# Score steps at other places of the block, and half of the probability masks on VectorE, in a hybrid pooling, convolution and attention layer

## The chip, the cores and the metric

The kernel runs on one core of one Trainium2 chip. The metric is the device time of one execution in microseconds. All matrix work is done in pairs of rounded values: each float32 operand is split into a high part and the rest (`hi` and `lo`), and a product is the sum of hi·hi, lo·hi and hi·lo.

## The reference

One layer over 4096 tokens of width 1024, with three groups of heads side by side. Only the attention group is touched by the change:

```
h = rms_norm(x, ln_g)
proj = h @ w_in                      # 1024 x 2816, split into u, g_pool, a, b, g_conv, q, k, v, g_attn
y_pool = pool_mixer(...)             # trailing means of 2/4/8/16 tokens
y_conv = conv_module(...)            # 31 taps, layer norm, silu, pointwise
# q: 8 heads of 64, k and v: 2 heads; each block of 128 queries sees its own and the previous 128 keys
scores = q_block @ [k_previous, k_own] * 64**-0.5 + alibi      # banded: 0 <= distance < 128
p = softmax(concat(scores, sink))[..., :-1]
y_attn = p @ [v_previous, v_own]
y = concat(y_pool * silu(g_pool), y_conv * silu(g_conv), y_attn * silu(g_attn))
out = rms_norm(x + y @ w_out, final_g)
```

## The kernel before

The program has three stages, one after the other. Each engine runs a list of its own, written out by hand, and waits on semaphores; no scheduler moves anything. The first stage (until about 656 us) is the **attention stage**, and only it is changed. Then come the mixer stage (projections of the pooling and convolution groups) and the output projection.

The attention stage goes over 8 blocks `n` of 512 tokens. In a block TensorE makes ten projections by `project`: `k`, `q0` to `q3`, `v`, and the gates `g0` to `g3`, each of 24 matmuls of 512 columns (8 slices `kk` of the 1024 inputs, three products each). The four q projections go to the PSUM tile `wide`, the others in turn to two banks `pair0` and `pair1`. It makes scores by `scores(n, j)` for four subtiles `j` of 128 queries, and the product of probabilities and values by `attend(n, batch)` for two subtiles at a time.

The way of one subtile goes over all engines:

- `scores` on TensorE, into the same PSUM tile as the q projections (tile `wide`).
- `take_scores(n, j, kv)` on VectorE, for 4 heads at a time: a predicated copy (L1034), four sums with the bias and a row maximum (L1038), and two small instructions (L1043, L1044).
- `exps` on ScalarE (L906, L909), `invert` on VectorE (L1055, L1058), `normalise` on GpSimd (L845).
- `turn_squares_of_probs` on VectorE (L1063) transposes the probabilities in squares of 32; `store_probs` and `load_probs` on the SP queue write them to DRAM (L690) and read them back turned (L699).
- `mask(n, j)` on GpSimd zeroes what lies outside the band: four instructions on 64 partitions x 512 columns (L855, L856, twice), two for the early and two for the late half of the queries. The semaphore `masked` counts them, and `attend` waits for it.
- `output(n, batch)` on VectorE multiplies the result by the gate (L1183) and writes `y_out`.

The input of the next block is prepared inside the block: `st.load` loads x, `square` (ScalarE) and `square_more` (VectorE) sum the squares, `fold_sums` is a small matmul on TensorE (L276) placed inside a projection, `mean` on VectorE and `root` on GpSimd (L288) follow, then `scale` on ScalarE (L294) and `turn_squares` on VectorE (L301) for four parts, then `split_hi` on ScalarE (L333) and `split_lo` on VectorE (L339) for 8 slices. The tile `xT` has one buffer: slice `kk` of the next block may be written only when `g3` of this block has read it (semaphore `spent`), and the next block's `k` reads slice by slice what is written.

In blocks 1 to 6 the combinations of the output weights (`combos`, 28 items, up to five a block) are made beside this: a sum on VectorE (L488), the high part on ScalarE (L496), the rest on VectorE (L500), and a store from SP (L506). Their staging tile has two buffers, so an item waits for the landing of the store of the item two before it.

The order in a block of TensorE: `k`, `q0`, `attend(n-1, 0)`, `q1`, `q2` (with the fold in it), `q3`, `v`, `attend(n-1, 1)`, then `scores(n, j)` and `g`j for j = 0 to 3, `turn_v` inside `scores(n, 1)`. Before the scores TensorE waits for all q rests (`q_taken`, made by `make_q_lo` on VectorE after `q_hi` on ScalarE). The last block ends with `attend(7, 0)`; `attend(7, 1)` stands in the mixer stage after its first two projections.

## Time and profile before

| what | value |
|---|---|
| time, median of 3 runs | 1454.54 us (1451.94 to 1455.07) |
| the profiled execution | 1452.87 us, its span 1450.7 us |
| TensorE matmul busy | 1363.4 us, 94% of the span |
| VectorE busy | 1170.9 us, 81% |
| ScalarE busy | 549.3 us, 38% |
| GpSimd busy | 504.8 us, 35% |
| DMA | mean 159 GB/s |

The span is the time from the first to the last instruction of the program; the device time of the same execution is 2.2 us more. Busy shares are means over the three stages. From 750 us on TensorE is busy nearly all the time; the idle time of TensorE lies in the attention stage, so the rows below are of that stage. A row of the timeline gives start, duration, engine, line, operation, and in brackets the idle time before and who ended it.

### The profile page before, as it was taken

How to read it: one execution, taken by the hardware profiler on the slowest of the kernel's cores; microseconds unless marked ns; L12 is line 12 of the kernel's file. 1: busy time of each engine (PE TensorE's matmuls, PEld its weight loads, DVE VectorE, ACT ScalarE, POOL GpSimd, SP SyncE). 2: the span in 40 equal slices, each digit the busy share in tenths (PEclk: the TensorE clock that was granted, in tenths of full speed). 3: DMA queues.
4: the chain of work that ended last, by engine and by line, in shares of the span. 5: the costliest groups of instructions: out<-in, count | busy, mean ns of one | idle time of the engine just before them, and what ended most of it. 6: DMA issues, size and time to landing. Idle time of an engine off the chain costs nothing.

```text
span 1450.7 us, 20622 instructions
## 1 busy us (share of the span) xinstructions
PE 1363.4 (94%) x7070; PEld 1112.5 (77%) x7070; DVE 1170.9 (81%) x2365; ACT 549.3 (38%) x1421; POOL 504.8 (35%) x640
## 2 busy tenths in 40 slices
PE   6989898989989899876999999999999999999998
PEld 5867676767778687755888888888888888888886
DVE  4877768685868675554989999989899998888886
ACT  5746555555555554330221221121222243333332
POOL 5254545445354534552010010110101255555552
PEclk9999999999999999988999999999999999999999
DMA  9757482939384736657031230330326756545531
GB/s 214 218 125 263 124 284 89 288 110 268 124 254 153 203 146 162 245 130 222 12 131 54 108 131 24 136 130 14 131 88 250 286 193 213 164 158 163 159 126 73
DMA packets 112426, 230.78 MB, mean 159 GB/s; under 512 B 16464, under 2 KB 74192, under 8 KB 104656
## 3 DMA queue, kind: packets, MB, share of 16 engines
q1 hardware_dynamic: 88192, 205.85, 42.5%
q10 hardware_dynamic: 24144, 23.80, 6.8%
q8 instruction: 49, 0.80, 0.2%
q14 instruction: 41, 0.34, 0.1%
HBM read 131.05 MB, written 98.57 MB: 158 GB/s over the span
## 4 chain that ended last, share of the span: by engine, by line
PE 66%; DVE 14%; DMA 8%; ACT 5%; POOL 3%; issue 2%; SPq 1%; POOLq 0%; ACTq 0%; DVEq 0%
PE wide L346 12%; PE wide L347 12%; PE wide L348 12%; DMA xs<-in_x_dram 5%; PE pair L1239 3%; PE pair L1233 3%; PE pair L1234 3%; DVE m_tail L1994 3%; DVE a_rows L1038 2%; ACT a_rows L909 2%; PE wide L1233 2%; PE wide L1234 2%; PE turn L1202 2%; PE wide L1239 2%; PE turn L347 2%
## 5 line engine op out<-in xcount | busy, mean ns | idle before, releaser
L1994 DVE SCALAR_TENSOR_TENSOR m_tail<-m_tail,m_taps 128x512 f32<-128x512 f32 x480 | 338.5, 750 | 4.6
L1233 PE MATMUL pair<-xT,w_hi 128*128 128x512 f32 x384 | 154.5, 402 | 27.0 <-ACT xT L333 23.5
L845 POOL TENSOR_SCALAR a_rows<-a_rows,a_inv 128x128 f32<-128x128 f32 x256 | 108.4, 443 | 204.1 <-DVE a_inv L1058 204.0
L1736 POOL TENSOR_TENSOR operand_sums<-m_y 128x512 f32<-128x512 f32 x75 | 102.2, 1362 | 167.7 <-PE wide L348 116.6
L108 POOL TENSOR_TENSOR pool_carrier<-pool_carrier 128x1 f32<-128x1 f32 x23 | 14.0, 611 | 394.5 <-DVE m_meanvar L2003 394.5
L1234 PE MATMUL pair<-xT,w_lo 128*128 128x512 f32 x384 | 150.8, 393 | 0.0
L1239 PE MATMUL pair<-xT,w_hi 128*128 128x512 f32 x384 | 149.2, 394 | 0.9 <-DVE xT L339 0.7
L346 PE MATMUL wide<-x_first,w_hi 128*128 128x512 f32 x320 | 125.4, 392 | 0.0
L346 PE MATMUL wide<-xT,w_hi 128*128 128x512 f32 x320 | 125.2, 391 | 0.0
L348 PE MATMUL wide<-x_first,w_hi 128*128 128x512 f32 x320 | 124.6, 389 | 0.0
L348 PE MATMUL wide<-xT,w_hi 128*128 128x512 f32 x320 | 124.5, 389 | 0.0
L347 PE MATMUL wide<-x_first,w_lo 128*128 128x512 f32 x320 | 124.5, 389 | 0.0
L347 PE MATMUL wide<-xT,w_lo 128*128 128x512 f32 x320 | 124.5, 389 | 0.0
L1233 PEld LDWEIGHTS pair<-xT,w_hi 128*128 128x128 f32 x384 | 72.5, 189 | 51.4 <-ACT xT L333 20.5
L1823 ACT ACTIVATE x_first<-operand_sums 128x512 fp32r<-128x512 f32 x80 | 50.5, 633 | 153.9 <-POOL operand_sums L1736 152.6
L1233 PE MATMUL wide<-xT,w_hi 128*128 128x512 f32 x256 | 103.9, 406 | 0.0
L1234 PE MATMUL wide<-xT,w_lo 128*128 128x512 f32 x256 | 102.5, 400 | 0.0
L1239 PE MATMUL wide<-xT,w_hi 128*128 128x512 f32 x256 | 102.1, 399 | 0.0
L909 ACT ACTIVATE a_rows<-a_rows,a_negmax 128x128 f32<-128x128 f32 x256 | 98.8, 387 | 0.0
L1239 PEld LDWEIGHTS pair<-xT,w_hi 128*128 128x128 f32 x384 | 72.5, 189 | 20.2 <-DVE xT L339 5.2
L1234 PEld LDWEIGHTS pair<-xT,w_lo 128*128 128x128 f32 x384 | 72.6, 189 | 12.3
L1038 DVE CUSTOM_DVE_ANT_0 a_rows<-wide,a_bias,a_sinks 128x128 f32<-128x128 f32 x256 | 74.6, 349 | 2.3
(262 smaller groups left out, 3233.8 us busy)
## 6 DMA issues: line engine op xcount, KB each, us to landing
xT_scratch<-xT SPq DMA_DIRECT2D x16, 2048.0 KB, 10.3
p_scratch<-a_rows SPq DMA_DIRECT2D x32, 512.0 KB, 2.6
x_first<-xT_scratch SPq DMA_DIRECT2D x16, 1024.0 KB, 8.7
xT<-xT_scratch SPq DMA_DIRECT2D x16, 1024.0 KB, 9.0
combo_scratch<-stage SPq DMA_DIRECT2D x28, 512.0 KB, 5.3
m_y<-y_scratch ACTq DMA_DIRECT2D x14, 1024.0 KB, 6.6
xs<-in_x_dram SPq DMA_DIRECT2D x20, 512.0 KB, 10.7
a_pT<-p_scratch SPq DMA_DIRECT2D x64, 128.0 KB, 4.7
```

The costliest lines, as they stand in the source:

```text
L346: nc.tensor.matmul(out, w_hi, x_hi, start=first, stop=False)
L347: nc.tensor.matmul(out, w_lo, x_hi, start=False, stop=False)
L348: return nc.tensor.matmul(out, w_hi, x_lo, start=False, stop=last)
L845: last = nc.gpsimd.tensor_scalar(probs[b][:, h], probs[b][:, h], inv[:, b, h:h + 1], 0.5, ALU.mult, ALU.mult)
L909: last = nc.scalar.activation(probs[b][:, h], probs[b][:, h], ACT.Exp, bias=negmax[:, b, h:h + 1], accum_out=rowsum[:, b, h:h + 1])
L1038: last = nc.vector.tensor_tensor_reduce(out=probs[b][:, h], in0=in_runs(score[:, h, P:]), in1=in_runs(bias[:, h]), scale=1.0, scalar=sinks ...
L1233: nc.tensor.matmul(out, w.hi(c)[:, kk, cols], st.hi[:, kk, :], start=(kk == 0), stop=False)
L1234: nc.tensor.matmul(out, w.lo(c)[:, kk, cols], st.hi[:, kk, :], start=False, stop=False)
L1239: last = nc.tensor.matmul(out, w.hi(c)[:, kk, cols], st.lo[:, kk, :], start=False, stop=(kk == KT - 1))
L1736: nc.gpsimd.tensor_tensor(operand_sums[:, i, 1], y_block(q, left), y_block(q, right), SIGN[op]).then_inc(operand_sum, 1)
L1823: nc.scalar.activation(operands[:, i, 0], operand_source(q, i), ACT.Copy).then_inc(operand_hi, 1)
L1994: nc.vector.scalar_tensor_tensor(out=conv[:, i, :], in0=h[:, i, j:j + TB], scalar=taps[:, i, j:j + 1], in1=conv[:, i, :], op0=ALU.mult, op ...
```

## The change

Four things are moved, all in the attention stage.

**TensorE.** `attend(n-1, 0)` comes before `q0` instead of after it. `scores(n, 0)` comes right after `q3`, before `attend(n-1, 1)` and `v`. `scores(n, 1)` stands in the middle of `g0`, `scores(n, 2)` after `g1`, `scores(n, 3)` in the middle of `g3`, and the next block's `k` at the end of the body. In the last block the scores of 1, 2, 3 stand before `g0`, `g1`, `g2`. The fold is moved from `q2` to `q3`.

**Masks.** GpSimd keeps the two instructions for the early queries (`mask_early`), and `mask_late` on VectorE makes the other two. Both add to `masked`, whose count per subtile stays two. On GpSimd the masks of subtiles 0 and 1 stand after `normalise` of 1 and 2, those of 2 and 3 ahead of `root`.

**VectorE and ScalarE** get a new order for the rest of the block: `output` directly after `make_k_lo`, the late masks of 2 and 3 among the q rests, the four `turn_squares` of x in the gates' part of the block instead of among the q rests, `scale` on ScalarE likewise, the first four splits ahead of the last subtile's scores, the other four behind it, as before.

**SP** stores the probabilities of subtile 3 after it has loaded those of subtile 2, and loads x first.

```diff
@@ SP, body(n)
+                st.load(sp, n + 1, (0, 1))
+                load_probs(sp, n - 1, 2)
                 store_probs(sp, n - 1, 3)
-                st.load(sp, n + 1, (0, 1))
-                for j in (2, 3):
-                    load_probs(sp, n - 1, j)
+                load_probs(sp, n - 1, 3)
@@ GpSimd
-        def mask(n, j):
+        def mask_early(n, j):
             m, b = SUB * n + j, j % 2
             pool.wait_ge(p_loaded[b], 16 * RUNS * (m // 2 + 1))
-            for late in range(2):
-                part = runs(whole[b][:, late * D // 2:(late + 1) * D // 2], halves[late])
-                nc.gpsimd.tensor_tensor(runs(rest[b], halves[late]), part, over_heads(rest_mask, halves[late]), ALU.mult)
-                nc.gpsimd.tensor_tensor(part, part, over_heads(whole_mask, halves[late]), ALU.mult).then_inc(masked, 1)
-                pool.wait_ge(masked, 2 * m + late + 1)
+            part = runs(whole[b][:, 0:D // 2], halves[0])
+            nc.gpsimd.tensor_tensor(runs(rest[b], halves[0]), part, over_heads(rest_mask, halves[0]), ALU.mult)
+            nc.gpsimd.tensor_tensor(part, part, over_heads(whole_mask, halves[0]), ALU.mult).then_inc(masked, 1)
@@ ScalarE, body(n), for the blocks between the first and the last
+            if not final:
+                st.scale(act, n + 1, 0)
+            for kv in range(KV):
+                exps(n, 0, kv)
+            take_v()
+            if not final:
+                st.scale(act, n + 1, 1)
+            for kv in range(KV):
+                exps(n, 1, kv)
+            spread_v()
+            gate_tanh(n, 0)
+            if not final:
+                st.scale(act, n + 1, 2)
+                gate_tanh(n, 1)
+                exps(n, 2, 0)
+                exps(n, 2, 1)
+                st.scale(act, n + 1, 3)
+                gate_tanh(n, 2)
+                for kk in range(st.AHEAD):
+                    st.split_hi(act, n + 1, kk)
+                exps(n, 3, 0)
+                gate_tanh(n, 3)
+                exps(n, 3, 1)
@@ VectorE, body(n)
             make_k_lo(n)
+            if not first:
+                output(dve, n - 1, 0)
                 turn_squares_of_probs(SUB * n - 1)
...
-                if t == 1 and not first and not final:
+                if t == 3 and not final:
                     st.mean(dve, n + 1)
                 make_q_lo(n, t)
...
                 make_combos(n, (t,) if t < 3 else (3, 4))
+                if t > 1 and not first:
+                    mask_late(dve, n - 1, t)
...
+            take_scores(n, 0, 0)
+            take_scores(n, 0, 1)
             if not first:
                 output(dve, n - 1, 1)
+            inverts(0)
+            next_x(0)
+            take_scores(n, 1, 0)
+            turn_squares_of_probs(SUB * n)
+            take_scores(n, 1, 1)
+            next_x(1)
+            inverts(1)
+            gate_make(n, 0)
+            if not final:
+                next_x(2)
+                gate_make(n, 1)
+                take_scores(n, 2, 0)
+                turn_squares_of_probs(SUB * n + 1)
+                take_scores(n, 2, 1)
+                inverts(2)
+                mask_late(dve, n, 0)
+                next_x(3)
+                gate_make(n, 2)
+                for kk in range(PIECE):
+                    st.split_lo(dve, n + 1, kk)
+                for kv in range(KV):
+                    take_scores(n, 3, kv)
+                turn_squares_of_probs(SUB * n + 2)
+                mask_late(dve, n, 1)
+                gate_make(n, 3)
+                inverts(3)
@@ the end of VectorE's attention program
         output(dve, NB - 1, 0)
+        for j in (2, 3):
+            mask_late(dve, NB - 1, j)
+
+    def mask_late(dve, n, j):
+        m, b = SUB * n + j, j % 2
+        dve.wait_ge(p_loaded[b], 16 * RUNS * (m // 2 + 1))
+        part = runs(whole[b][:, D // 2:], halves[1])
+        nc.vector.tensor_tensor(runs(rest[b], halves[1]), part, over_heads(rest_mask, halves[1]), ALU.mult)
+        nc.vector.tensor_tensor(part, part, over_heads(whole_mask, halves[1]), ALU.mult).then_inc(masked, 1)
@@ TensorE, body(n)
-                project(n, "k")
-                project(n, "q0")
                 attend(pe, n - 1, 0)
-            for name in ("q1", "q2", "q3", "v"):
-                project(n, name, folding(n) if name == ("q3" if first else "q2") and not final else None)
+            for name in ("q0", "q1", "q2", "q3"):
+                project(n, name, folding(n) if name == "q3" and not final else None)
             pe.wait_ge(q_taken, GROUP * (n + 1))
+            scores(n, 0)
             if not first:
                 attend(pe, n - 1, 1)
-            for j in range(SUB):
-                scores(n, j, turn_v if j == 1 else None)
-                project(n, f"g{j}")
+            project(n, "v")
+            if final:
+                scores(n, 1, lambda: turn_v(n))
+                project(n, "g0")
+                scores(n, 2)
+                project(n, "g1")
+                scores(n, 3)
+                project(n, "g2")
+                project(n, "g3")
+                attend(pe, n, 0)
+            else:
+                project(n, "g0", halfway(lambda: scores(n, 1, lambda: turn_v(n))))
+                project(n, "g1")
+                scores(n, 2)
+                project(n, "g2")
+                project(n, "g3", halfway(lambda: scores(n, 3)))
+                project(n + 1, "k")
```

Three places show what this does to the order. The first is TensorE after the last q projection of a block. Before, `v` (in `pair`) and the 32 products of `attend` (L1202) stand between `q3` and the scores (L1262, L1271):

```order
L1239 MATMUL pair<-xT,w_hi 128x512
L1202 MATMUL turn<-a_pT,a_v 64x128 x8
L1202 MATMUL turn<-a_rows,a_v 64x128 x8
L1202 MATMUL turn<-a_pT,a_v 64x128 x8
L1202 MATMUL turn<-a_rows,a_v 64x128 x8
L1262 MATMUL wide<-a_k_lo,a_q 128x256 x8
L1271 MATMUL wide<-a_k_hi,a_q 128x256 x8
```

Now the scores (L1294, L1303) follow the last matmul of `q3` (in `wide`), and `attend` (L1234) follows them:

```order
L1271 MATMUL wide<-xT,w_hi 128x512
L1294 MATMUL wide<-a_k_lo,a_q 128x256 x8
L1303 MATMUL wide<-a_k_hi,a_q 128x256 x8
L1234 MATMUL turn<-a_pT,a_v 64x128 x8
L1234 MATMUL turn<-a_rows,a_v 64x128 x8
L1234 MATMUL turn<-a_pT,a_v 64x128 x8
L1234 MATMUL turn<-a_rows,a_v 64x128 x8
L1265 MATMUL pair<-xT,w_hi 128x512
```

So nothing stands any more between `q3` and the scores, which need its rests. The second place is VectorE from the rests of `q3` (`a_q`) to the first scores of the block. Before:

```order
L1083 SCALAR_TENSOR_TENSOR a_q<-wide,a_q 64x512 x2
L301 STREAM_TRANSPOSE xs<-xs 128x1024
L488 TENSOR_TENSOR stage_sum<-raw 128x512 x2
L500 TENSOR_TENSOR stage<-stage_sum,stage 128x512 x2
L301 STREAM_TRANSPOSE xs<-xs 128x1024
L1183 TENSOR_TENSOR y_out<-turn,a_gate 128x2x4x64 x2
L1034 COPY_PREDICATED wide<-a_rows,wide 128x4x128
```

Now, with the late masks of subtile 2 (L1205, L1206, in `a_pT`) and of subtile 3 (in `a_rows`):

```order
L1205 TENSOR_TENSOR a_pT<-a_pT,a_rows 64x512
L1206 TENSOR_TENSOR a_pT<-a_pT,a_rows 64x512
L282 TENSOR_SCALAR a_meansq<-turn 128x16
L1084 SCALAR_TENSOR_TENSOR a_q<-wide,a_q 64x512 x2
L488 TENSOR_TENSOR stage_sum<-raw 128x512 x2
L500 TENSOR_TENSOR stage<-stage_sum,stage 128x512 x2
L1205 TENSOR_TENSOR a_rows<-a_rows 64x512
L1206 TENSOR_TENSOR a_rows<-a_rows 64x512
L1035 COPY_PREDICATED wide<-a_rows,wide 128x4x128
```

The two combinations stay where they were, and the mask of subtile 3, for which `attend(n-1, 1)` waits, stands behind them. The third place is VectorE at the turn from one block to the next. Before, behind the last scores, with the splits of the next block's x (L339):

```order
L1063 STREAM_TRANSPOSE a_rows<-a_rows 128x1024
L339 SCALAR_TENSOR_TENSOR xT<-xs,a_gain,xT 128x512
L1093 SCALAR_TENSOR_TENSOR a_gate<-a_tanh,pair 128x512
L339 SCALAR_TENSOR_TENSOR xT<-xs,a_gain,xT 128x512 x3
L1055 TENSOR_TENSOR a_denom<-a_rowsum,a_sinkexp 128x4
L1058 RECIPROCAL a_inv<-a_denom 128x4
L339 SCALAR_TENSOR_TENSOR xT<-xs,a_gain,xT 128x512 x4
L1063 STREAM_TRANSPOSE a_rows<-a_rows 128x1024
```

Now, behind the last scores:

```order
L1064 STREAM_TRANSPOSE a_rows<-a_rows 128x1024
L1205 TENSOR_TENSOR a_rows<-a_rows 64x512
L1206 TENSOR_TENSOR a_rows<-a_rows 64x512
L1094 SCALAR_TENSOR_TENSOR a_gate<-a_tanh,pair 128x512
L1056 TENSOR_TENSOR a_denom<-a_rowsum,a_sinkexp 128x4
L1059 RECIPROCAL a_inv<-a_denom 128x4
L1056 TENSOR_TENSOR a_denom<-a_rowsum,a_sinkexp 128x4
L1059 RECIPROCAL a_inv<-a_denom 128x4
L339 SCALAR_TENSOR_TENSOR xT<-xs,a_gain,xT 128x512 x4
L1071 COPY a_k_lo<-a_k_lo 128x2x128
```

The first four splits have moved ahead of the last subtile's scores; the last four stand behind both of its scores, a transpose, a mask and a gate.

## Rows read from the trace of the kernel before

**Rows 1.** The waits of TensorE, 50 to 720 us: total us, times, longest

```profile
PE turn L1202 <- POOL a_rows L856: 25.6, 3, 11.1
PE pair L1233 <- ACT xT L333: 23.5, 14, 1.7
PE turn L276 <- ACT a_tanh L239: 13.7, 6, 2.7
```

**Rows 2.** Timeline of TensorE at a block's turn: start, duration, x count, idle before

```profile
319.26 0.47 PE L1233 MATMUL pair<-xT,w_hi 128*128 128x512 f32 x1 [1.61 <-ACT xT L333]
...
323.73 0.50 PE L1233 MATMUL pair<-xT,w_hi 128*128 128x512 f32 x1 [1.74 <-ACT xT L333]
...
327.59 0.40 PE L1233 MATMUL wide<-xT,w_hi 128*128 128x512 f32 x1
...
333.17 1.09 PE L1202 MATMUL turn<-a_pT,a_v 128*64 128x128 f32 x16
...
336.11 0.50 PE L1233 MATMUL wide<-xT,w_hi 128*128 128x512 f32 x1
...
345.96 0.36 PE L276 MATMUL turn<-a_sumsq,a_fold 128*128 128x16 f32 x2 [2.74 <-ACT a_tanh L239]
```

**Rows 3.** Timeline of TensorE at the first scores of block 3

```profile
287.47 0.73 PE L1262 MATMUL wide<-a_k_lo,a_q 64*128 64x256 f32 x8
...
289.19 0.39 PE L1233 MATMUL pair<-xT,w_hi 128*128 128x512 f32 x1
```

**Rows 4.** ScalarE's first instruction behind `k`, all blocks: min/median/max ns, first and last start

```profile
L934 ACT ACTIVATE a_k_hi<-a_k_hi x7: 417/418/421, 95.8 to 560.6; 128x256 fp32r<-128x256 f32 x7
```

**Rows 5.** A stretch behind a fold: length, busy us PE, PEld, DVE, ACT, POOL, granted clock, DMA

```profile
190.10:193.50 3.40, 3.40 (x10) 2.73 (x11) 2.26 (x5) 1.47 (x3) 2.71 (x1) 0.50 1.06 454
```

**Rows 6.** Timeline of TensorE, the last two products of probabilities and values

```profile
640.24 1.98 PE L1202 MATMUL turn<-a_pT,a_v 128*64 128x128 f32 x16 [9.53 <-POOL a_rows L856]
...
667.28 1.98 PE L1202 MATMUL turn<-a_pT,a_v 128*64 128x128 f32 x16 [11.11 <-POOL a_rows L856]
```

**Rows 7.** Groups of VectorE, 0 to 650 us: x count, busy us, mean ns, idle before

```profile
L1038 DVE CUSTOM_DVE_ANT_0 a_rows<-wide,a_bias,a_sinks 128x128 f32<-128x128 f32 x256 | 74.6, 349 | 2.3
L1083 DVE SCALAR_TENSOR_TENSOR a_q<-wide,a_q 64x512 fp32r<-64x512 f32 x64 | 44.1, 689 | 39.2 <-ACT a_q L898 38.0
L1034 DVE COPY_PREDICATED wide<-a_rows,wide 128x512 f32<-128x512 uint32 x62 | 42.2, 681 | 0.0
L339 DVE SCALAR_TENSOR_TENSOR xT<-xs,a_gain,xT 128x512 fp32r<-128x512 f32 x56 | 40.2, 769 | 0.0
L1063 DVE STREAM_TRANSPOSE a_rows<-a_rows 128x1024 f32<-128x1024 f32 x32 | 39.5, 1234 | 8.6 <-POOL a_rows L845 8.6
L301 DVE STREAM_TRANSPOSE xs<-xs 128x1024 f32<-128x1024 f32 x28 | 34.4, 1231 | 1.5 <-ACT xs L294 1.3
...
L488 DVE TENSOR_TENSOR stage_sum<-raw 128x512 f32<-128x512 f32 x20 | 15.6, 778 | 6.1 <-DMA combo_scratch<-stage 3.7 <-DMA raw<-in_w_out_dram 2.0
L500 DVE TENSOR_TENSOR stage<-stage_sum,stage 128x512 fp32r<-128x512 f32 x20 | 15.1, 754 | 11.2 <-ACT stage L496 11.0
```

**Rows 8.** Groups of ScalarE, 0 to 650 us

```profile
L909 ACT ACTIVATE a_rows<-a_rows,a_negmax 128x128 f32<-128x128 f32 x256 | 98.8, 387 | 0.0
...
L294 ACT ACTIVATE xs<-xs,a_rstd 128x256 f32<-128x256 f32 x112 | 47.5, 496 | 1.6 <-POOL a_rstd L288 1.3
...
L333 ACT ACTIVATE xT<-xs,a_gain 128x512 fp32r<-128x512 f32 x56 | 35.7, 709 | 0.0
```

**Rows 9.** A mask group of GpSimd, 0 to 690 us

```profile
L856 POOL TENSOR_TENSOR a_pT<-a_pT,a_rows 64x512 f32<-64x512 f32 x32 | 41.0, 1280 | 0.0
```

**Rows 10.** Timeline of VectorE among the combinations of block 3

```profile
277.26 1.35 DVE L500 TENSOR_TENSOR stage<-raw,stage 128x512 fp32r<-128x512 f32 x1 [1.48 <-ACT stage L496]
...
284.05 0.69 DVE L488 TENSOR_TENSOR stage_sum<-raw 128x512 f32<-128x512 f32 x1 [0.98 <-DMA combo_scratch<-stage]
```

**Rows 11.** The combination's store issued at 264.4 us beside xT's: x count, KB, us to landing

```profile
xT_scratch<-xT SPq DMA_DIRECT2D x1, 2048.0 KB, 10.7
combo_scratch<-stage SPq DMA_DIRECT2D x1, 512.0 KB, 11.6
```

More of the change, by code:

```diff
@@ L957, in body @@
             q_hi(n, 2)
-            if not first and not final:
-                st.scale(act, n + 1, 0)
             for s in combos.of_block(n, (2,)):
@@ L965, in body @@
                 w.split_hi(act, CHUNK_CB)
[L966 to L967 removed]
             q_hi(n, 3)
[L969 to L971 removed]
+            for s in combos.of_block(n, (3, 4)):
                 combos.split_hi(act, s)
@@ L1284, in folding, with turn_v, halfway @@
             return once
+        def turn_v(n):
+            pe.wait_ge(free(slot("v")), earlier(n, slot("v")) + 1)
+            need(pe, gated, batches_before(n, 0))
+            for s in range(SUB):
+                last = nc.tensor.transpose(turn[1][:, s * P:(s + 1) * P], vT[:, s * P:(s + 1) * P], ident[:])
+            last.then_inc(v_turned, 1)
+        def halfway(action):
+            return lambda kk: action() if kk == KT // 2 - 1 else None
         def body(n):
-            first = isinstance(n, int) and n == 0
+            first, final = n == 0, n == NB - 1
             if first:
```

153 lines of the change are left out of this document (55 added, 98 removed).

## The prediction

> **What bounds the kernel now.** I read first the busy shares: TensorE is the fullest engine, and its gaps are all in the attention stage. So the next view is who ends TensorE's waits there [rows 1]: the masks on GpSimd (25.6 us, three waits at the end of the stage), the splits of x at each block's turn (23.5 us), the fold (13.7 us). The timeline shows them in place [rows 2]: `k` waits 1.61 and 1.74 us for ScalarE's splits, the fold 2.74 us for the squares. A block lasts (560.6 - 95.8)/6 = 77.5 us [rows 4]. Its own work on TensorE is ten projections of 5.5 us (327.59 to 333.17 is one), two `attend` of 2.9 (333.17 to 336.11) [rows 2], four scores of 1.7 (287.47 to 289.19) [rows 3] and 0.6 for turning `v`: 68.4 us. The other 9 us are the waits and the clock: behind a fold's wait the granted clock is 0.50 for 3.4 us [rows 5], that is 1.2 instead of 2.4 GHz and some 1.6 us lost, in four blocks. At the end `attend` waits 9.53 and 11.11 us [rows 6], and runs at the low clock again.
>
> **The change, worked out over one block.** Set K = 0 where `k`'s last matmul ends, and follow a block from 1 to 5 until the next K. The sum is made against the profiled execution, 1452.9 us (1.7 us under the median).
>
> *TensorE to the end of q3.* 2.9 for `attend(n-1, 0)`, four projections 22.1, the fold 0.3: 25.3. The fold stands 5.5 us later, and the longest wait for it was 2.74 [rows 2], so it costs nothing now: x is still loaded at the block's turn. Its cover is gone only if x lands more than 3 us later than before. Gain 2.3 us a block, and the low clock with it.
>
> *The rests of q3.* Before, `v` and an `attend` (8.4 us) covered them. Now the scores follow at once and need ScalarE's two copies and VectorE's two rests (0.69 each [rows 7]): with the copies first, 2.1 us of idle time at least, scores at 27.4 to 29.1.
>
> *What VectorE does around it.* Between the rests of q3 and the mask of subtile 3 stand two combinations: four instructions of 0.7 to 0.8 (L488, L500 [rows 7]), then the late mask. No row shows a mask on VectorE. The nearest are the two-input instructions of 512 columns there, 0.69 to 0.75 on average and 1.35 for the one that ran beside GpSimd's masks [rows 7, 10]; against GpSimd's 1.28 [rows 9]. I take 0.68, 1.35 for the pair, since GpSimd has finished its own by then; the bounds are 1.3 and 2.7. That ends the mask at 27.3 + 2.7 + 1.35 = 31.3 if nothing waits, and `attend(n-1, 1)`, which TensorE could start at 29.1, waits 2.2.
>
> *The store that comes into it.* A combination waits for the landing of the store two before it. The block's first store is issued behind 2 MB of xT and lands 11.6 us later [rows 11]. SP now comes to it after the load of subtile 3, which waits for that subtile's store; I put it at 15, its landing at 26.3. The third combination then starts at 26.3 instead of 22.4, and it stands ahead of q3's rests on both engines: the scores slip to 31.3. The fifth waits for the third's store (one such wait of 0.98 shows before [rows 10]), and the mask ends at 37.1. So `attend(n-1, 1)` starts between 31.3 and 37.1; from there 2.9 + 5.5 (`v`) + 2.75 (half of g0) = 11.2 to `scores(n, 1)`.
>
> *From scores(n, 1) to the next K.* TensorE's own work is 30.4 us: the scores with `v` 2.2, half of g0 2.75, g1 5.5, scores 1.7, g2 5.5, g3 with scores 7.2, k 5.5. VectorE's list in the same stretch: 1.3 until the first scores are there; six `take_scores` of 2.07 (0.68 + 4 x 0.35 with the overlaps and two small ones) 12.4; three transposes of probabilities and three of x at 1.15 net, 6.9; two masks 2.7; four gates 2.6; eight splits of 0.72 (0.77 on average, beside GpSimd) 5.8; the inverses 1.5: 33.2 [rows 7]. In it are four waits for ScalarE that nothing covers: for the exponentials of the scores just taken (4 x 0.39 + 0.2 each) before the two inverses, 0.6 and 1.8, for the tanh behind the turned `v` 1.0, for a scale (4 x 0.5) 0.9 [rows 8]: 4.3. Together 37.5. The last splits, which `k` must have, stand behind the last scores, a transpose, a mask and a gate. So `k` ends 7.1 us later than TensorE alone would make it, against about 4.4 before. VectorE's 5.4 us of masks a block lie on this path; GpSimd, which is relieved of them, was off it.
>
> The period is then 31.3 + 11.2 + 37.4 = 79.9 without store waits, 85.7 with them. The landing of 11.6 us [rows 11] makes the second the nearer; I take 84.5, that is 7.0 us more than 77.5 in each of five blocks: +35. Block 6 has no fourth and fifth combination: +0.2 to +4, I take +3. Block 0: `root` (2.9 us) now comes after the last weights, and the scale is ahead of the first exponentials: +5.
>
> *The last block and the end.* The wait before `attend(6, 1)` goes (the weights' loads have one projection more to pass), `attend(7, 0)` has two projections more between it and its scores: I count 2.1 for q3's rests, 1.1 for scores 3, 3.8 before `attend(7, 0)` (the mask behind the last gate), 8.6 before the last one. The last is 11.11 [rows 6] less two mask instructions of 1.28 [rows 9]; its loads are issued as late as before. That is 15.6 for 31.4 (25.6 of waits [rows 1], 5.3 of low clock, 0.5), with some 2 of low clock left: -14, between -10 and -18.
>
> The sum: 35 + 3 + 5 - 14 = **+29 us**, at the median 1484.
>
> *A rule of the chip's notes.* VectorE's instruction with two SBUF inputs took 1.35 us beside GpSimd's masks instead of about 0.7 [rows 10]. The Trainium skill, page "SBUF — State Buffer", section "Who interferes with whom", says the same: an instruction of VectorE with two SBUF inputs contends with one of GpSimd that reads SBUF, and one waits for the other to end. The late masks are of this form, so moving them makes them such a rival of what GpSimd keeps. By that rule one of a block's four masks, that of subtile 0 (GpSimd scales probabilities then), would take up to 1.3 us more: 7 times, +9 at most.
>
> **The rivals.**
>
> *The stores don't hold it* (xT is through before the combinations need the buffer). Then +2.4 x 5 + 0.2 + 5 - 14 = +3, 1458. For it: the third and fourth stores landed in 3 to 6 us. Against it: the first, 11.6 [rows 11], whose place is the one that counts.
>
> *Faster.* If the chain of 37.5 us is hidden to the extent that `k` waits only as long as before (4.4), and the stores don't hold, the blocks come to 77.2, and only the end shows: -14 to -20, 1438. The point from which it decides is a period of 77.5 + 14/6.5 = 79.6 us. Were `k` not held at all (72.8 us a block), 1412. For it: the waits for ScalarE were estimated, and the before's splits had ScalarE's exponentials in front of them too. Against it: VectorE's instructions alone are 33.2 us where TensorE has 30.4.
>
> *The clock.* Idle times of 5 to 7 us in a block would each bring 3.4 us at 0.50 right where TensorE is late (behind `k`, and at `v`); after 2.7 us it fell too [rows 5]. At 1.6 us each, 6 to 12 of them add 10 to 19: 1500.
>
> **How the numbers follow.** The forecast, 1470 to 1497, has 0.53; with the clock or the contention on top, up to 1508, 0.16; the free stores, 1455 to 1465, 0.15, of which 0.03 is within 0.2%; faster 0.13; unchanged by cancelling, 0.03. A measurement of this kernel can tell about 0.2% (3 us) from no change. That gives faster 0.13, same 0.06, slower 0.81. The predicted time is the forecast's, 1484. The range from 1454 to 1508 leaves out the faster cases and some 5% above.
>
> **What would show it.** In the changed kernel's trace: starts of L928 (ScalarE's first copy behind `k`) more than 80 us apart; a wait of TensorE of 5 us or more inside `k` for ScalarE's splits; one of 2 us or more before the block's first scores, ended by VectorE's rests; one before `attend(n-1, 1)` ended by a mask on VectorE, which in block 6 is small; no wait at the fold; masks on VectorE of about 0.7 us. The prediction is wrong if the period is under 79.6, that is if either the splits come in time or the stores land before the combinations ask for them.

## The result

The changed kernel takes **1529.7 us** (median of 4 runs, 1525.1 to 1534.6) against 1454.8 in the same sessions: 1.052 times as long, 95% interval 1.048 to 1.056. The sign was right; the time lies 22 us above the range. The profiled execution has a span of 1523.4 us against 1450.7: +72.7 where the sum said +29.

Who ends TensorE's waits now, 50 to 760 us (total, times, longest; it answers to [rows 1]):

```profile
PE pair L1265 <- ACT xT L333: 57.6, 7, 8.7
PE turn L1234 <- DVE a_rows L1206: 30.1, 6, 7.1
PE wide L1294 <- DVE a_q L1084: 27.1, 8, 5.1
PE turn L1234 <- POOL a_rows L855: 6.9, 1, 6.9
PE turn L276 <- DVE a_sumsq L248: 1.9, 4, 0.5
```

All three waits that the prediction named are there: `k` for ScalarE's splits, `attend(n-1, 1)` for the mask on VectorE, the first scores for q3's rests; the fold's wait is down to 1.9 us. The blocks are longer than forecast, by ScalarE's first copy behind `k` (to [rows 4]):

```profile
L928 ACT ACTIVATE a_k_hi<-a_k_hi x7: 417/418/419, 106.5 to 646.4; 128x256 fp32r<-128x256 f32 x7
```

Block 0 ends at 106.5 us instead of 95.8 (its first scores wait 4.3 us, its `k` 7.8). Blocks 1 to 5 take 91.4 us each, where 84.5 was forecast, block 6 takes 82.7, and from block 7's K to the end the execution is 13.1 us shorter. 10.7 + 5 x 13.9 + 5.2 - 13.1 = 72.3, rounding apart the 72.7; of each block's 13.9 us the forecast has 7.0.

Where a block's other 6.9 us lie, in block 2 (K = 198.4). First TensorE in `k` (start, duration, count, idle before), then three stretches (length, busy PE, PEld, DVE, ACT, POOL, granted clock, DMA share, GB/s):

```profile
275.62 0.39 PE L1271 MATMUL pair<-xT,w_hi 128*128 128x512 f32 x1
284.39 0.79 PE L1265 MATMUL pair<-xT,w_hi 128*128 128x512 f32 x1 [8.39 <-ACT xT L333]
284.99 0.63 PE L1266 MATMUL pair<-xT,w_lo 128*128 128x512 f32 x1
```

```profile
276.10:279.80 3.70, 0.00 (x0) 0.00 (x0) 3.63 (x15) 0.00 (x0) 0.00 (x0) 1.00 0.00 0
284.40:286.80 2.40, 2.40 (x6) 1.92 (x7) 2.30 (x8) 1.78 (x3) 1.30 (x3) 0.50 0.36 145
286.80:290.00 3.20, 3.20 (x9) 2.52 (x8) 1.95 (x3) 0.00 (x0) 3.20 (x6) 0.50 0.01 1
```

TensorE stands 8.39 us, and nearly all that is left of `k` then runs at a granted clock of 0.50 (1.2 GHz): 15 matmuls in 6.4 us, which take 3.4 at full clock. Most of this runs while VectorE still makes the last splits (VectorE, ScalarE's first copy behind `k`):

```profile
285.58 3.16 DVE L339 SCALAR_TENSOR_TENSOR xT<-xs,a_gain,xT 128x512 fp32r<-128x512 f32 x4
290.82 0.42 ACT L928 ACTIVATE a_k_hi<-a_k_hi 128x256 fp32r<-128x256 f32 x1 [4.64 <-PE pair L1271]
```

The last split ends at 288.7, so `k` ends 2.1 us behind it (2.0 in the mean of blocks 1 to 5, 0.9 in the kernel before). `attend(1, 1)`, behind a wait of 5.57 us, takes 4.3 us instead of 2.9. In the whole execution 132.7 us are at 0.50, against 44.5 before.

VectorE in the same block, at the squares of the next x and at the combinations, with GpSimd beside the squares:

```profile
215.94 1.51 DVE L248 CUSTOM_DVE_ANT_0 a_pT<-xs 128x256 f32<-128x256 f32 x1
...
217.39 1.50 DVE L248 CUSTOM_DVE_ANT_0 a_pT<-xs 128x256 f32<-128x256 f32 x1
...
218.82 0.41 DVE L248 CUSTOM_DVE_ANT_0 a_pT<-xs 128x256 f32<-128x256 f32 x1
...
234.09 0.69 DVE L500 TENSOR_TENSOR stage<-raw,stage 128x512 fp32r<-128x512 f32 x1 [4.03 <-ACT stage L496]
234.81 0.69 DVE L1205 TENSOR_TENSOR a_rows<-a_rows 64x512 f32<-64x512 f32 x1
```

```profile
215.71 1.46 POOL L854 TENSOR_TENSOR a_rows<-a_rows 64x512 f32<-64x512 f32 x1 [3.33 <-DMA a_rows<-p_scratch]
217.14 1.47 POOL L855 TENSOR_TENSOR a_rows<-a_rows 64x512 f32<-64x512 f32 x1
```

Two squares take 1.5 us instead of 0.42, each until just after a mask instruction of GpSimd has ended. The rests of q stand behind them on VectorE; how much of that reaches the first scores is seen below in the run without these masks. Further down, the fifth combination stands 4.03 us for the landing of a store, and the mask of subtile 3 (L1205, 0.69 as forecast) stands behind it. By groups, 0 to 750 us (mean ns in the second number behind the bar; the low splits took 769 before [rows 7], the squares 422):

```profile
L339 DVE SCALAR_TENSOR_TENSOR xT<-xs,a_gain,xT 128x512 fp32r<-128x512 f32 x56 | 53.4, 1012 | 1.9 <-ACT xT L333 1.9
L248 DVE CUSTOM_DVE_ANT_0 a_pT<-xs 128x256 f32<-128x256 f32 x56 | 30.8, 615 | 0.2
```

### The profile page after: what moved, and what is told of

Its sections match the earlier page's. It is cut to its first block, busy times and chain, and to the rows that moved or that the text cites. A ratio compares the mean times of both kernels' runs of the same rounds, so it can differ in the third digit from the quotient of the medians.

```text
span 1523.4 us, 20599 instructions
## 1 busy us (share of the span) xinstructions
PE 1379.3 (91%) x7070; PEld 1133.5 (74%) x7070; DVE 1217.8 (80%) x2429; ACT 547.4 (36%) x1421; POOL 426.0 (28%) x576
## 4 chain that ended last, share of the span: by engine, by line
PE 49%; DVE 6%; ACT 1%; issue 1%; SPq 1%; DMA 0%; POOL 0%; POOLq 0%; DVEq 0%; ACTq 0%
PE wide L346 11%; PE wide L347 11%; PE wide L348 11%; DVE m_tail L2038 3%; PE turn L346 2%; PE pair L346 2%; PE pair L348 2%; PE turn L348 2%; PE pair L347 2%; PE turn L347 2%; PE turn L1234 1%; DVE x_first L2135 1%; DVE a_rows L1039 1%; PE wide L1265 0%; PE wide L1271 0%
## 5 line engine op out<-in xcount | busy, mean ns | idle before, releaser
L1265 PE MATMUL pair<-xT,w_hi 128*128 128x512 f32 x384 | 159.5, 415 | 61.0 <-ACT xT L333 57.6
L1266 PE MATMUL pair<-xT,w_lo 128*128 128x512 f32 x384 | 156.9, 409 | 0.0
L1271 PE MATMUL pair<-xT,w_hi 128*128 128x512 f32 x384 | 154.8, 413 | 0.0
L1265 PEld LDWEIGHTS pair<-xT,w_hi 128*128 128x128 f32 x384 | 76.2, 199 | 81.3 <-ACT xT L333 61.3
L346 PE MATMUL wide<-xT,w_hi 128*128 128x512 f32 x320 | 125.2, 391 | 0.0
L348 PE MATMUL wide<-xT,w_hi 128*128 128x512 f32 x320 | 124.5, 389 | 0.0
L1265 PE MATMUL wide<-xT,w_hi 128*128 128x512 f32 x256 | 101.4, 396 | 0.0
L1271 PE MATMUL wide<-xT,w_hi 128*128 128x512 f32 x256 | 99.7, 390 | 0.0
L1271 PEld LDWEIGHTS pair<-xT,w_hi 128*128 128x128 f32 x384 | 78.2, 204 | 17.9 <-DVE xT L339 0.2
L1266 PEld LDWEIGHTS pair<-xT,w_lo 128*128 128x128 f32 x384 | 76.6, 199 | 14.6
L1035 DVE COPY_PREDICATED wide<-a_rows,wide 128x512 f32<-128x512 uint32 x62 | 42.3, 682 | 45.1 <-PE wide L1303 44.9
```

What stands on the lines that cost most here:

```text
L346: nc.tensor.matmul(out, w_hi, x_hi, start=first, stop=False)
L348: return nc.tensor.matmul(out, w_hi, x_lo, start=False, stop=last)
L1035: nc.vector.copy_predicated(score[:, heads, P:], for_heads(earlier_tile.bitcast(mybir.dt.uint32)), earlier_keys).then_inc(take_step, 1)
L1265: nc.tensor.matmul(out, w.hi(c)[:, kk, cols], st.hi[:, kk, :], start=(kk == 0), stop=False)
L1266: nc.tensor.matmul(out, w.lo(c)[:, kk, cols], st.hi[:, kk, :], start=False, stop=False)
L1271: last = nc.tensor.matmul(out, w.hi(c)[:, kk, cols], st.lo[:, kk, :], start=False, stop=(kk == KT - 1))
```

## The experiments

Theory at this point: the loss is the order's (VectorE's last splits behind too long a chain, a store ahead of a mask), made larger by GpSimd's masks beside VectorE's two-input instructions and by the low clock behind the new waits. The rivals: the masks on VectorE themselves; VectorE's work as a whole. "Ratio" is to the kernel before in the same session. "Block" is the mean period of blocks 1 to 5 and "end" the time from block 7's K to the last instruction, both in the profiled execution. K is read from ScalarE's first copy behind `k`, except in the three runs with a star: there exponentials stand ahead of that copy, it starts 6.8 us after `k`'s last matmul, and K is read from that matmul.

| run | us | ratio (95%) | block | end |
|---|---|---|---|---|
| before | 1454.8 | 1 | 77.5 | 890.1 |
| changed | 1529.7 | 1.052 (1.048 to 1.056) | 91.4 | 877.0 |
| a1_order_alone | 1541.5 | 1.058 (1.056 to 1.060) | 92.2 | 885.5 |
| a2_mask3_first | 1499.6 | 1.029 (1.026 to 1.031) | 85.5 | 879.8 |
| a3_no_port | 1510.9 | 1.037 (1.036 to 1.039) | 89.4 | 876.4 |
| a4_fill | 1522.8 | 1.046 (1.044 to 1.048) | 90.3 | 878.9 |
| b1_masks_alone | 1457.2 | 1.003 (1.001 to 1.004) | 79.7 | 881.9 |
| b3_fold_later | 1475.4 | 1.015 (1.012 to 1.018) | 82.0 | 891.0 |
| b4_final_order | 1452.0 | 0.999 (0.997 to 1.000) | 77.7 | 887.0 |
| b5_end_only | 1445.8 | 0.994 (0.992 to 0.996) | 77.7 | 880.0 |
| d1_splits_ahead * | 1501.4 | 1.033 (1.030 to 1.036) | 86.9 | 883.8 |
| e0_queue_alone | 1487.0 | 1.021 (1.018 to 1.023) | 84.0 | 880.4 |
| d2_queue * | 1450.4 | 0.996 (0.995 to 0.998) | 77.7 | 887.4 |
| d3_refined * | 1438.5 | 0.988 (0.986 to 0.989) | 75.9 | 886.4 |

### Order or masks: each alone

The new order with all masks on GpSimd (in `mask_early`; `mask_late` is empty):

```
+            for late in range(2):
+                part = runs(whole[b][:, late * D // 2:(late + 1) * D // 2], halves[late])
+                nc.gpsimd.tensor_tensor(runs(rest[b], halves[late]), part, ...)
+                nc.gpsimd.tensor_tensor(part, part, ...).then_inc(masked, 1)
```

> The new order with all masks back on GpSimd, early and late half of each subtile together, at the places of the early ones. Theory (the order is the loss, the masks on VectorE are a small part): VectorE loses 1.4 us per mask, four masks per block; of these one lies ahead of the turned squares that open attention on the odd batch and two on the chain from the first scores to the next block's last splits, so some 3 to 4 us per block go, while GpSimd's masks stay beside VectorE's squares and splits for longer: 1529.7 - 15 to 25 = 1505 to 1515. Rival 1 (the masks on VectorE, with their waits for the stores' landing, are most of the loss): 1455 to 1475. Rival 2 (GpSimd, with twice the masks, sets the end of attention instead): 1530 or more, with waits of TensorE put down to POOL.

It is 12 us slower than the changed kernel. That is the time of the second rival, but not its cause: TensorE hardly waits for GpSimd (50 to 760 us),

```profile
PE pair L1262 <- ACT xT L333: 72.5, 7, 10.5
PE turn L276 <- DVE a_sumsq L248: 16.4, 6, 3.2
PE turn L1231 <- POOL a_rows L856: 1.2, 1, 1.2
```

and longer than in the changed kernel for what comes behind VectorE's splits (72.5 us for 57.6) and squares (16.4 for 1.9). VectorE loses its own masks, but its groups (as above) show what it pays:

```profile
L339 DVE SCALAR_TENSOR_TENSOR xT<-xs,a_gain,xT 128x512 fp32r<-128x512 f32 x56 | 67.4, 1261 | 3.2 <-ACT xT L333 3.2
L248 DVE CUSTOM_DVE_ANT_0 a_pT<-xs 128x256 f32<-128x256 f32 x56 | 46.6, 893 | 0.2
```

Splits and squares take 29.8 us more than in the changed kernel, two thirds of what VectorE's masks cost there (32 masks of 1.4 us, 46); so VectorE has less work in all, but more of it stands ahead of `k` and of the fold. In block 2 four squares take 1.5 us, beside four mask instructions; in the changed kernel two beside two. Between the two profiled executions the difference is 20 us, 8.5 of it at the end and 5.7 in block 6. The other half, the old order with the late masks on VectorE (the masks of subtiles 0 and 1 stand further down):

```
...
+                if t == 3 and not first:
+                    mask_late(dve, n - 1, t)
                 make_combos(n, (t,) if t < 3 else (3, 4))
+                if t == 2 and not first:
+                    mask_late(dve, n - 1, t)
...
```

> The kernel before, in its old order, with only the late halves of the masks moved to VectorE (subtile 2 after the third combos, 3 ahead of the last combos, 0 after the last scores, 1 behind the last splits). Theory (the masks on VectorE are not what costs; the order is): GpSimd's shorter masks stretch fewer of VectorE's squares and splits, which gives back about the 1.4 us that each mask takes; within 6 us of the time before: 1449 to 1462. Rival (masks on VectorE stand in its chains and cost 1 to 2 us each, 25 masks): 1475 to 1500.

+0.3%: the block is 2.2 us longer, the end 8.2 shorter: blocks 1 to 6 lose about 12 us and the end gives most of it back. So **the whole loss is the order's**; moving masks costs next to nothing in the old order and gives 12 us in the new.

### The store ahead of the mask

```
+                if t == 3 and not first:
+                    mask_late(dve, n - 1, t)
                 make_combos(n, (t,) if t < 3 else (3, 4))
-                if t > 1 and not first:
+                if t == 2 and not first:
                     mask_late(dve, n - 1, t)
```

> In the changed kernel VectorE masks subtile 3 of the previous block ahead of the last two combos of q instead of behind them. Theory: the fifth combo waits 4.0 us for the landing of a store, and the mask, the turned squares and attention on the odd batch stand behind it (the wait of 30.1 us in six blocks); with the mask in front attention on that batch starts 4 to 6 us earlier in each of six blocks, and the scores behind it too: 1529.7 - 24 to 33, and a few us more where TensorE's clock then stays up: 1495 to 1505. Rival (the wait before attention on the odd batch is VectorE's own length of work, not the store): the combos move behind the mask and hold the q rests or the next work, no more than 8 us gained: 1522 to 1530.

30 us less, as expected: the 30.1 us of waits before `attend` for VectorE's masks shrink to one of 5.2, at the end of the stage (the one for GpSimd there grows from 6.9 to 8.9). The wait in `k` is untouched (58.1 us).

### GpSimd beside VectorE

This run leaves most of the early masking out of the computation, so it is a measurement and no usable kernel:

```
-            part = runs(whole[b][:, 0:D // 2], halves[0])
-            nc.gpsimd.tensor_tensor(runs(rest[b], halves[0]), part, over_heads(rest_mask, halves[0]), ALU.mult)
...
+            nc.gpsimd.tensor_tensor(rest[b][halves[0], 0:HD], whole[b][halves[0], 0:HD], rest_mask[halves[0]], ALU.mult)
...
```

> The changed kernel with GpSimd's early masks cut to one head's 64 columns (most of the early masking is left out of the computation). Theory: GpSimd's masks beside VectorE's two-input instructions stretch the squares of the next x from 2.9 to 4.9 us and four low splits from 2.8 to 4.6 us; without them about 1.9 us of the gap ahead of the first scores and 1.8 us of the wait in k go in each of six blocks, with some of the low clock behind: 1529.7 - 23 to 30 = 1500 to 1507. Rival (no contention; the long instructions have another cause): the time stays within 5 us of 1529.7, and the squares still take 4.9 us.

18.8 us less (14.2 between the two profiled executions), 4 short of the theory and far from the rival. The two groups are nearly back at their lengths of before:

```profile
L339 DVE SCALAR_TENSOR_TENSOR xT<-xs,a_gain,xT 128x512 fp32r<-128x512 f32 x56 | 41.5, 799 | 1.9 <-ACT xT L333 1.9
L248 DVE CUSTOM_DVE_ANT_0 a_pT<-xs 128x256 f32<-128x256 f32 x56 | 21.2, 444 | 0.2
```

VectorE saves 21.5 us here, 11.9 at the splits and 9.6 at the squares, but not at the two places where the theory had put the gain in equal parts. From K to `attend(n-1, 1)` a block is only 0.7 us shorter, and the waits ahead of the first scores stay (27.8 us for 27.1); from `scores(n, 1)` to the next K it is 1.9 shorter. So the splits are on the path and the squares hardly. Up to 1.9 us are GpSimd's own, at the one wait for its mask (6.9 to 5.0). The Trainium skill, page "SBUF — State Buffer", section "Who interferes with whom", calls this an exclusive lock on a shared port; the one square per mask instruction, held until that ends, agrees.

### The clock

Matmuls whose results nobody reads keep TensorE busy in its long waits, at three places; one of them is

```
+                    if kk == PIECE and n > 0:
+                        need(pe, gated, 2 * (n - 1))
+                        fill(0, FILL_K)
                     pe.wait_ge(st.hi_done, KT * n + kk + 1)
...
```

> The changed kernel with matmuls that compute nothing needed, put into TensorE's long waits: 8 ahead of the first scores, 12 ahead of attention on the odd batch, 30 ahead of the late slices of k, per block. Theory: the waits keep their ends, but the stretches at a granted clock of 0.50 behind them (132.7 us in all, against 44.5 us before the change) shrink; of the 88 us more at half clock some 2 us per block lie on the chain through attention on the odd batch and 1 to 2 us in the rest of k: 1529.7 - 15 to 27 = 1503 to 1515, mean granted clock back near 0.98. Rival (the low clock costs nothing, since TensorE waits for VectorE anyway): within 5 us of 1529.7, or slower by the fillers' own time (up to 3 us per block, 1545).

Only 6.9 us less (3.2 between the two profiled executions, with 55.1 us at 0.50 instead of 132.7). In `k` the fillers did their work: the rest of block 2's `k` runs at full clock,

```profile
280.20:285.20 5.00, 4.35 (x17) 2.79 (x19) 4.35 (x10) 1.89 (x4) 3.80 (x6) 1.00 0.18 73
```

but in 5.0 us, not 3.4, since at that pace it catches up with VectorE's low splits (12 new waits of at most 0.3 us). So of the 3 us that `k` loses at the low clock about one was to be had (the third part of a block is 0.9 us shorter); the rest hides behind the splits. Ahead of `attend(n-1, 1)` the run says less: the part from there to `scores(n, 1)` falls to 11.3 us in blocks 2, 4 and 5, but `attend` starts later, 37.3 us after K in the mean of the blocks instead of 36.8, in blocks 2 and 4 without any wait, so the fillers themselves stand in its way. 6.9 us is what this run gave back, not all that the clock costs.

### The parts of the order in the old kernel

First the fold in `q3`, with the mean, the root, the scaling and the turned squares behind it, and one mask of GpSimd moved ahead of the root:

```
-                project(n, name, folding(n) if name == ("q3" if first else "q2") and not final else None)
+                project(n, name, folding(n) if name == "q3" and not final else None)
...
+                mask(n - 1, 2)
             if n < NB - 1:
                 st.root(pool, n + 1, carrier)
             if n > 0:
-                for j in (2, 3):
-                    mask(n - 1, j)
+                mask(n - 1, 3)
```

> The kernel before with only the fold of the next x's squares moved from q2 to q3, and with it the mean, the root, the scaling and the turned squares that follow. The wait ahead of the fold (13.7 us before, with low clock behind it) goes. Theory (a gain of this part is real, but its followers move to VectorE's chain from the scores to the next splits, which already makes TensorE wait 20.2 us in k): 1455 - 14 to 20, less up to 6 back through the wait in k: 1437 to 1447. Rival (the followers come late altogether, the wait in k grows by more than the fold's wait gave): 1460 to 1475.

The fold's wait is gone, and the kernel is 20 us slower, as the rival said, but at another place than it said: TensorE's waits for GpSimd's masks rise from 25.6 to 54.7 us, because I left the mask of subtile 3 behind the root and the root waits for the later mean (GpSimd, block 2):

```profile
204.52 2.91 POOL L288 TENSOR_TENSOR a_rstd<-a_meansq,a_power 128x16 f32<-128x16 f32 x1 [4.82 <-DVE a_meansq L282]
207.40 1.29 POOL L855 TENSOR_TENSOR a_rows<-a_rows 64x512 f32<-64x512 f32 x1
```

This run prices my placing of the mask, not the later fold alone.

For the end, the last block's new order alone (with ScalarE's and VectorE's lists of that block to match), and then that with the last six subtiles' late masks on VectorE:

```
-            for name in ("q1", "q2", "q3", "v"):
+            for name in ("q1", "q2", "q3") if final else ("q1", "q2", "q3", "v"):
...
+            if final:
+                scores(n, 0)
             if not first:
                 attend(pe, n - 1, 1)
+            if final:
+                project(n, "v")
...
```

> The kernel before with only the last block in the changed kernel's order (scores one and a half projections apart, the first scores ahead of attention on the odd batch), masks still on GpSimd. Theory (the 13.1 us that the end gains in the changed kernel come from this order): 1455 - 9 to 14 = 1441 to 1446. Rival (they come from the late masks on VectorE, which unburden GpSimd at the end): 1452 to 1458.

```
-            for late in range(2):
+            for late in range(1 if m >= SUB * (NB - 1) - 2 else 2):
...
```

> The kernel before with the last block in the changed kernel's order and with the late halves of the masks on VectorE only for the last six subtiles that attention reads. Theory (the 13.1 us that the changed kernel's end gives are some 3 us of order and some 10 us of masks that two engines share, since the waits there, 5.0, 9.5 and 11.1 us, end with GpSimd's masks): the end as in the changed kernel, 98.5 us against 111.6, blocks as before: 1442 +- 3. Rival (in the old blocks GpSimd comes to the end as late as before): 1450 to 1455.

The order gives 3.1 us of the end in the trace (its ratio's interval includes 1), both together 10.1: the masks are the larger part, as in b1 (8.2). So b4 missed what its theory expected and came out as its rival, and b5 ended 1 us above its range. It is 0.6% faster than the kernel before.

### Where the last splits stand

The wait in `k` was left. In this run, made from a2, all eight splits stand ahead of the last scores' work on both engines, the mask of subtile 1 goes with them on VectorE, and ScalarE's squares get a wait of their own for the gate:

```
                 for kk in range(st.AHEAD):
                     st.split_hi(act, n + 1, kk)
+                act.wait_ge(proj_full, filled(n, slot("g3")))
+                for kk in range(st.AHEAD, KT):
+                    st.split_hi(act, n + 1, kk)
                 exps(n, 3, 0)
...
-                for kk in range(PIECE):
+                for kk in range(KT):
                     st.split_lo(dve, n + 1, kk)
+                mask_late(dve, n, 1)
                 for kv in range(KV):
                     take_scores(n, 3, kv)
```

> The changed kernel with the mask of subtile 3 ahead of the last combos, and with all eight splits of the next x ahead of the last scores' own work on ScalarE and VectorE (before, the second four stood behind the scores of subtile 3, their exponentials and the gate). Theory (what holds k is the place of these four splits on VectorE's and ScalarE's chain, 41.9 us from the second scores to the end of k against 30.4 us of TensorE's own): k's wait goes nearly whole, the end of k comes some 33 us after the second scores, period 85.5 - 8 = 77.5 or less: 1499.6 - 6 x 8 = 1452, down to 1440 where the low clock behind the wait goes too. Rival (VectorE's work as a whole is the bound of the block, so that what is put behind k returns as a wait ahead of the first scores or of attention): 1480 to 1500.

The wait in `k` is gone (2.4 us in all, the longest 0.2), and nothing is gained (1501.4 against 1499.6): it has moved to the first scores, up to 13.8 us,

```profile
PE wide L1300 <- DVE a_q L1088: 64.1, 8, 13.8
```

which looks like the rival, VectorE's work as a whole. But VectorE stands idle in the stretch (block 3, where `k` ends at 271.3):

```profile
292.69 0.43 DVE L248 CUSTOM_DVE_ANT_0 a_pT<-xs 128x256 f32<-128x256 f32 x1 [2.84 <-issue]
...
306.63 0.69 DVE L500 TENSOR_TENSOR stage<-raw,stage 128x512 fp32r<-128x512 f32 x1 [5.56 <-ACT stage L496]
```

and the queue of SyncE (start, duration of the issues, count) tells why:

```profile
277.55 0.34 SPq L690 DMA_DIRECT2D p_scratch<-a_rows  x1
277.93 1.94 SPq L189 DMA_DIRECT2D xs<-in_x_dram  x2
285.92 1.86 SPq L699 DMA_DIRECT2D a_pT<-p_scratch  x4
287.88 1.75 SPq L690 DMA_DIRECT2D p_scratch<-a_rows  x1
295.39 1.73 SPq L699 DMA_DIRECT2D a_rows<-p_scratch  x4
297.30 0.36 SPq L733 DMA_DIRECT2D xT_scratch<-xT  x1
297.70 2.35 SPq L506 DMA_DIRECT2D combo_scratch<-stage  x2
```

x was free at 270.7 (the last low split's end), but SyncE's half of its load stood behind a store of probabilities and went out at 277.9 (ScalarE's half, behind exponentials, at 276.4); its last part landed at 292.6, when the squares begin. The first combination, ready at 288.4, waits behind the load of subtile 3, which waits until 295.4 for its store, and then goes out behind 2 MB of xT. It lands at 305.9, and the combination that needs its buffer stood until then. ScalarE's first copy behind `k` also starts later than the end of `k` here, which is why the table goes by the matmul:

```profile
270.80 0.50 PE L1277 MATMUL pair<-xT,w_hi 128*128 128x512 f32 x1 [0.16 <-DVE xT L339]
278.08 0.41 ACT L928 ACTIVATE a_k_hi<-a_k_hi 128x256 fp32r<-128x256 f32 x1
```

The next run puts SyncE's issues in another order, and issues ScalarE's half of the load right behind ScalarE's last split too:

```
-                st.load(sp, n + 1, (0, 1))
                 load_probs(sp, n - 1, 2)
                 store_probs(sp, n - 1, 3)
-                load_probs(sp, n - 1, 3)
+            for s in combos.of_block(n, (0,)):
+                combos.store(sp, s)
+            if n > 0:
+                load_probs(sp, n - 1, 3)
             store_xT(n, 0)
...
+            if n + 2 < NB:
+                st.load(sp, n + 2, (0, 1))
             store_probs(sp, n, 2)
```

> The run with the eight splits ahead of the last scores (1501.4 us), with SyncE's queue reordered: the next x is loaded by both queues right behind its last split instead of after the exponentials and the store of the probabilities (landed 20 us after the start of attention there, the squares waited 2.8 us for it), and the first combo is stored ahead of the wait for the last probabilities (it lay ready 9 us, and its landing held the fourth combo for 5.6 us). Theory (SyncE's queue in its order is what holds VectorE's chain to the first scores): 8 to 10 us of the wait ahead of the first scores go in each of six blocks, period 87 - 9 = 78 down to 75, with less low clock: 1430 to 1455. Rival (VectorE's own work in that stretch is the bound): 4 us or less per block, 1478 to 1500.

51 us less, and faster than the kernel before by 0.4%. Is it the queue alone? Nearly the same reordering without the splits' move (x cannot be loaded as early then: SyncE's half goes behind the last store of probabilities, and ScalarE's half stays where it was):

> The run with the mask of subtile 3 first (1499.6 us), with only SyncE's queue reordered (the first combo stored ahead of the wait for the last probabilities, the first store of xT behind them), the splits left behind the last scores. Theory (VectorE's chain from the first scores to the last splits and SyncE's queue are two bounds, one behind the other, and the splits' place alone gave nothing because the queue came next): the wait in k stays at 8 us per block, the wait ahead of the first scores shrinks by 1 to 3 us: 1482 to 1497. Rival (the queue was the whole of it, and the splits' place is worth nothing): 1450 to 1460.

12.6 us, and the wait in `k` stays (58.5 us in 7). So there were two bounds, one behind the other: the splits' place is worth -1.8 us (it costs) with the old queue and 36.6 with the new, the queue 12.6 and 51. The 36.6 and the 51 hold the earlier load of x as well, which no run shows alone.

### The last run

Two more moves on top of d2, the mask of subtile 2 on VectorE and the second store of xT on SyncE:

```
                 if t == 3 and not first:
+                    mask_late(dve, n - 1, 2)
                     mask_late(dve, n - 1, t)
                 make_combos(n, (t,) if t < 3 else (3, 4))
-                if t == 2 and not first:
-                    mask_late(dve, n - 1, t)
...
-            store_xT(n, 1)
             for s in combos.of_block(n, (2, 3, 4)):
                 combos.store(sp, s)
+            store_xT(n, 1)
```

> The run with the splits ahead and the queue reordered (1450.4 us), with the mask of subtile 2 behind q's last rests and the second store of xT behind the combos' stores. Theory (the wait of 3 to 5 us ahead of the first scores is the length of VectorE's work between q2 and q3, and the mask's 1.4 us is in it; the store of xT holds the fifth combo's buffer for 4.5 us, behind which VectorE takes the first scores late): 1.4 us in each of seven blocks and a little from the first scores taken earlier: 1436 to 1442. Rival (attention on the odd batch then waits for the later mask): 1448 to 1453.

1438.5 us, 1.2% faster than the kernel before (0.9861 to 0.9894). A block takes 75.9 us, and over eight blocks 20.7 us of waits for q's rests are left, with 16.4 for the late masks:

```profile
PE wide L1304 <- DVE a_q L1093: 20.7, 8, 4.0
PE turn L1244 <- DVE a_rows L1216: 16.4, 13, 5.2
```

In this kernel `k`'s last matmul ends block 0 at 97.3 us instead of 95.4; blocks 1 to 5 are 1.6 us shorter each, block 6 2.3 and the end 3.7. What the new order has in this is not shown: the old order was never run with SyncE's queue re-sorted or with the splits ahead, and the small change b5 in the old order already reaches 1445.8.

## Why the prediction failed

**Right.** The mechanism and the sign: `k` behind VectorE's chain, the mask behind a store, q3's rests uncovered, late masks of 0.69 us, almost no wait at the fold (1.9 us in all), +5.2 in block 6 (+3 forecast), -13.1 at the end (-14). Wrong are sizes in the sum, as follows.

**The period, 91.4 for 84.5**, by the forecast's own three parts, means of blocks 1 to 5:

| part | forecast | measured |
|---|---|---|
| K to `attend(n-1, 1)` | 35.9 (31.3 to 37.1) | 36.8 |
| to `scores(n, 1)` | 11.2 | 12.9 |
| to the next K | 37.4 | 41.8 |

- *The first part* was sized well, with its places mixed up. In block 2 the first combination's store landed in 8.2 us and did not hold the third; the third's own store, issued beside the second store of xT, held the fifth. The squares, held 2 us by GpSimd, had no term in the sum, but count for little here: without GpSimd's masks this part is 0.7 us shorter.
- *The second part, 12.9 for 11.2: the clock.* The sum had zero for it, and a rival 10 to 19 us. Behind its wait `attend` takes 4.3 to 4.6 us instead of 2.9; in block 6, where it does not wait, the part takes 11.3. The step that failed is the choice to add the parts at full clock after finding idle times of 5 to 7 us in front of them, when a wait of 2.74 had already shown 0.50 [rows 2, 5].
- *The third part, 41.8 for 37.4: the length of the splits, and `k` behind them.* The last low split ends 39.8 us after `scores(n, 1)`, where the sum had 37.5. The sum took L339 at 0.72; four of them took 4.6 us instead of 2.8 beside GpSimd's masks. The rule of the Trainium skill, page "SBUF — State Buffer", section "Who interferes with whom", was weighed for one late mask, +9 at most, and not for the splits and the squares. The mean of L339 in [rows 7] was taken as a property of the instruction; it depends on what GpSimd does then, and the change moved that. Without GpSimd's masks this part is 1.9 us shorter. The other 2.0 us are `k` behind the last split, which the sum left out; it was 0.9 before, so about 1.1 may be put down to the low clock, near the 0.9 that the fillers gave back there.

By these places a block's 6.9 us are 0.9, 1.7 and 4.4, and of them the low clock has some 2.7 (an estimate from the rows above: 1.6 and 1.1) and GpSimd's masks beside VectorE 2.1, by the period of the run without them. The two runs that take one cause away gave 6.9 us (clock) and 18.8 us (GpSimd's masks, the larger of the two by this measure) of the whole; for the clock that is a lower bound, since the fillers also delayed `attend`.

**Block 0**, 10.7 for 5: the waits are 4.3 us for q3's rests, which the sum charges to every other block and I left out of this one, and 7.8 in `k`.

**The end**: the number was right, partly by luck: the forecast counted waits without saying what the order and what the masks give, and ahead of b4 I still expected all of it from the order. In the old kernel the masks alone give 8.2 and the order alone 3.1.

**The rivals.** Faster, at a period under 79.6 us, did not happen in this kernel; d2 and d3, with periods of 77.7 and 75.9, are faster. "The stores don't hold it" would have given +3; a2, in which the mask no longer stands behind the stores, is still 44 us slower than before, so it was wrong on its own. The clock's rival, 10 to 19 us, fits the estimate above (2.7 us in five blocks) better than the 6.9 us of the fillers.

Open: how much of a block's 2.2 us in b1 is the masks' own time and how much their places; what the later fold costs without the mask of subtile 3 behind the root; what the earlier load of x gives alone; and what the re-sorted queue gives in the old order.

## To carry over

A new order of one engine is only as good as the queues that feed it: follow each in-order queue (here SyncE's) from its first held instruction to what stands behind it, and re-sort it with the order. When a fix moves a wait without moving the time, look whether the engine that is now waited for is busy or idle; if it is idle, as VectorE was here for 5.56 us, look for what it waits for in turn. And a mean duration is a fact about the neighbours too: before using it, look what runs beside the instruction in the new order.

## What the hardware showed

- A square of VectorE whose two inputs are the same tile (L248) is held by GpSimd's mask like any other two-input instruction: 0.42 us alone, 1.5 beside one, in block 2 one square per mask instruction (two and two in the changed kernel, four and four in a1).
- In the wait of 8.39 us the granted clock was 1.00 up to 279.8 and then 0.50, and it stayed at 0.50 for the 5.6 us of work that followed (to 290.0).
- The same 512 KB store of a combination took 2.7 and 3.1 us to land in block 2 of the changed kernel when no store of xT was on its way, and 8.2 both times when it was issued less than 2 us behind the 2 MB of xT.
